# Two products of a recurrence placed beside two others, and each level's product spread over two banks

## The reference

```python
def step(s, inp):
    r_t, w_t, k_t, v_t, a_t, b_t = inp
    sa = jnp.einsum('bhvk,bhk->bhv', s, a_t)
    s = s * w_t[:, :, None, :] + sa[..., None] * b_t[:, :, None, :] + v_t[..., None] * k_t[:, :, None, :]
    y = jnp.einsum('bhvk,bhk->bhv', s, r_t) if emit else None
    return s, y
```

## Time and profile before

| | |
|---|---|
| Runs before, median (lowest to highest) | 2892.83 us (2891.24 to 2895.13), 3 runs |
| Profiled execution: its own time | 2893.22 us |
| its span, first to last instruction | 2891.4 us |
| granted TensorE clock, mean | 0.991 |
| TensorE busy | 2797.3 us, 29,030 products and as many weight loads |
| DVE, ScalarE busy | 1185.1 us, 683.0 us |

### The profile page before, as it was taken

How to read it: one execution, slowest core, us unless ns; L and a number is a source line. 1 busy time by engine, 2 the same in 40 slices (tenths; PEclk the granted TensorE clock), 3 DMA queues, 4 the chain that set the end, 5 groups by cost and what they waited for, 6 DMA issues and landing times.

```text
span 2891.4 us, 63725 instructions
## 1 busy us (share of the span) xinstructions
PE 2797.3 (97%) x29030; PEld 1683.3 (58%) x29030; DVE 1185.1 (41%) x2444; ACT 683.0 (24%) x1425; POOL 3.0 (0%) x7
## 2 busy tenths in 40 slices
PE   7999999999999999999999999989999999999997
PEld 4478777445777888864588787863333333333332
DVE  4777565445545444247786564431111011011101
ACT  2345312544322111013454126520000000000000
POOL 0000000000000000000000000000000000000000
PEclk9999999999999999999999999999999999999999
DMA  7100143212242433232000442459999999999995
GB/s 293 59 3 4 47 159 111 66 44 92 83 136 68 146 117 90 80 120 84 30 4 5 171 160 94 150 219 346 413 365 364 416 359 377 402 361 413 369 375 198
DMA packets 188787, 534.55 MB, mean 185 GB/s; under 512 B 6113, under 2 KB 80097, under 8 KB 171105
## 3 DMA queue, kind: packets, MB, share of 16 engines
q1 hardware_dynamic: 187440, 526.21, 48.6%
q0 software_dynamic: 1072, 4.19, 0.4%
HBM read 528.29 MB, written 2.10 MB: 183 GB/s over the span
## 4 chain that ended last, share of the span: by engine, by line
PE 92%; DVE 4%; ACT 1%; SPq 1%; issue 1%; DMA 1%; DVEq 0%; ACTq 0%
PE bank L572 68%; PE bank L700 12%; PE bank L1337 8%; PE bank L818 2%; PE bank L1199 1%; SPq L2990 1%; DVE WR L2456 1%; ACT ar L1627 0%; DMA rep<-in_repeated 0%; PE bank L923 0%; ACT WR L1627 0%; DVE RS L2330 0%; DVE AT L2127 0%; DVE ar L2389 0%; DVE WR L2437 0%
## 5 line engine op out<-in xcount | busy, mean ns | idle before, releaser
L572 PE MATMUL bank<-AT,WR 128*128 128x512 f32 (+1 forms) x1408 | 521.4, 521 | 5.9 <-ACT AT L1627 3.7
L1627 ACT ACTIVATE ar<-bank 128x256 f32<-128x256 f32 (+2 forms) x338 | 155.1, 463 | 1535.3 <-PE bank L572 1028.3
L572 PE MATMUL bank<-WR,ar 128*32 128x512 f32 (+1 forms) x4464 | 444.5, 555 | 1.6 <-DVE ar L2899 1.6
L572 PE MATMUL bank<-ar 128*32 128x512 f32 (+6 forms) x3990 | 429.6, 509 | 9.9 <-ACT ar L1627 5.9
L572 PEld LDWEIGHTS bank<-AT,WR 128*128 128x128 f32 x1408 | 263.0, 192 | 213.0 <-issue 196.9
L572 PEld LDWEIGHTS bank<-ar 128*32 128x32 f32 (+3 forms) x3990 | 176.1, 124 | 248.5 <-issue 237.3
L572 PEld LDWEIGHTS bank<-WR,ar 128*32 128x32 f32 x4464 | 143.7, 110 | 288.4 <-issue 285.8
L1627 ACT ACTIVATE WR<-bank 128x512 f32<-128x512 f32 (+1 forms) x224 | 122.8, 592 | 200.0 <-PE bank L572 174.7
L572 PE MATMUL bank<-AT,ar 128*32 128x512 f32 (+1 forms) x1456 | 151.5, 561 | 11.3 <-ACT AT L1627 11.3
L2909 DVE TENSOR_TENSOR YB<-YB,bank 128x512 f32<-128x512 f32 x28 | 18.0, 684 | 342.9 <-PE bank L572 342.9
L2917 DVE TENSOR_TENSOR ar<-ar,bank 128x512 f32<-128x512 f32 (+1 forms) x48 | 29.8, 621 | 286.9 <-PE bank L572 285.5
(11 more groups left out here) (368 smaller groups left out, 3287.6 us busy)
## 6 DMA issues: line engine op xcount, KB each, us to landing
WR<-in_moe_w_down SPq DMA_DIRECT2D x27, 2048.0 KB, 14.8
WR<-in_ada_w SPq DMA_DIRECT2D x20, 2048.0 KB, 8.0
ar<-in_moe_w_down SPq DMA_DIRECT2D x20, 2048.0 KB, 14.7
WR<-in_w_in SPq DMA_DIRECT2D x18, 2048.0 KB, 9.3
WR<-in_moe_w_gate SPq DMA_DIRECT2D x18, 2048.0 KB, 16.6
WR<-in_moe_w_up SPq DMA_DIRECT2D x15, 2048.0 KB, 15.9
WR<-in_moe_w_up SPq DMA_DIRECT2D x18, 1536.0 KB, 7.8
WR<-in_moe_w_gate SPq DMA_DIRECT2D x15, 1536.0 KB, 8.5
```

The lines of the kernel that those rows point to most:

```text
L572: return pe.matmul(o, lhsT, rhs, start=first, stop=last)
L1627: return act.activation(out, in_, func, **k)
```

## The change

`solve(i - 1)` is issued alternately with `level(i, 1)`, into bank 2 alone, from a third buffer `XT[2]`; the transposed values of chunk i are issued alternately with `level(i, 2)`, into bank 7. Both then use the two partition pairings that the level does not. The level's product goes to two banks, q 0 to 3 and q 4 to 7, and signals after each; `masked` is two instructions of half the width, and `inverse_doubled` waits for the first half before q = 0 and for the second before q = 4. Levels, grown and turned inverse go round over the banks 0, 1 and 6. The order within a chunk, on TensorE and on DVE, is another:

```diff
+        def level_banks(i, n):
+            return [banks[(0, 1, 6)[(5 * i + n + m) % 3]] for m in range(2)]
+        def grown_bank(i, n):
+            return banks[(0, 1, 6)[(5 * i + n + 2) % 3]]
+        def turned_bank(i, n):
+            return banks[(0, 1, 6)[(5 * i + n) % 3]]
+        solved_bank, gram_bank = banks[2], banks[7]
...
+                def value_turned(i, q, h):
+                    c = CH * (i if q < 4 else BWD[i])
+                    last = mm(pair(gram_bank, q, h), Rv[64 * h:64 * h + 64, q % 4, c:c + CH],
+                              eye[64 * h:64 * h + 64, 64 * h:64 * h + 64], True, True)
...
+                def solve(i, q, h):
+                    last = mm(pair(solved_bank, q, 1 - h), pair(XT[2], q, 1 - h), pair(G, q, 1 - h), True, True)
...
                     for q in range(8):
+                        bank = level_banks(i, n)[q // 4]
                         for h in range(2):
-                            ins = mm(pair(level_bank, q, 1 - h if n else h), pair(LTs[i % 2], q, h),
-                                     pair(X[n > 0], q, h), True, True)
-                            if (q, h) == (7, 1):
-                                ins.then_inc(S.full, 1)
+                            ins = mm(pair(bank, q, 1 - h if n else h), pair(LTs[i % 2], q, h), pair(X[n > 0], q, h), True, True)
+                        if q % 4 == 3:
+                            ins.then_inc(S.full, 1)
+                            S.done(("T1", l, i, n, q // 4))
+                        for h in range(2 if beside else 0):
+                            if beside == "solve":
+                                solve(i - 1, q, h)
+                            elif beside == "values":
+                                value_turned(i, q, h)
...
                 def inverse_doubled(i, n):
-                    pe.wait_ge(S.free, S.jobs[("T1", l, i, n)])
...
                     for q in range(8):
+                        if q % 4 == 0:
+                            pe.wait_ge(S.free, S.jobs[("T1", l, i, n, q // 4)])
...
                     if i:
                         level(i, 0)
-                        solve(i - 1)
                         inverse_doubled(i, 0)
+                        level(i, 1, "solve")
+                        inverse_doubled(i, 1)
                         y_of_chunk(i - 1, ybank)
-                        level(i, 1)
                         state(i - 1)
-                        inverse_doubled(i, 1)
-                        values_turned(i)
+                        level(i, 2, "values")
                         if i <= 4:
                             bonus(i - 1)
-                        level(i, 2)
+                        inverse_doubled(i, 2)
                         pe.wait_ge(responses_ready, seen(responses_ready))
                         against(i, 0)
-                        inverse_doubled(i, 2)
-                        against(i, 2)
                     level(i, 3, "X" if i < NCH - 1 else None)
-                    against(i, 4)
+                    against(i, 2 if i else 4)
                     inverse_doubled(i, 3)
-                    against(i, 6)
+                    against(i, 4 if i else 6)
                     level(i, 4, "LT" if i < NCH - 1 else None)
-                    if i == 0:
+                    if i:
+                        against(i, 6)
+                    else:
                         pe.wait_ge(uv_cleared, seen(uv_cleared))
                     ybank = from_state(i)
                     inverse_doubled(i, 4)
...
-                def masked(n):
-                    TT(dq(T1), step_product(banks[6]), mk(M_LEVEL + 1 + n), ALU.mult).then_inc(S.free, 1)
+                def masked(i, n):
+                    for d in range(2):
+                        bank = level_banks(i, n)[d]
+                        TT(dq(T1)[:, d], step_product(bank)[:, d],
+                           masks[:, M_LEVEL + 1 + n, d, :].unsqueeze(1).to_broadcast([128, 4, CH]), ALU.mult).then_inc(S.free, 1)
```

## The result

The changed kernel takes 2900.99 us (median of 16 runs, 2898.13 to 2904.14); the kernel before, on the same chip, 2892.85 (16 runs). The ratio is 1.0027, 95% interval [1.0020, 1.0035]: some 8 us slower, where 2882 was forecast. The profiled execution has a span of 2899.5 us against 2891.4.

The account below looks back on a forecast made before the run. TensorE's path was taken as the bound, with instruction packets a second limit (128 products each 3.5 to 4.1 us). Layer 0's -4.4 and layer 1's -6.4 us gave -10.8 from 2892.83: 2882 us, range 2870 to 2893.

Parts of the forecast that it names:

- the sum's addition for packets: Time added per chunk for TensorE's waits for instruction packets: 1.1 us without bonus work, 0.4 with, 0.3 to 0.7 elsewhere.
- The layout with its holes filled: Chunk schedule from level 0 to next level 0, before waits for packets: 20.8 us without bonus work, 22.5 with.
- both bounds: Limits on the time added for packet waits in a chunk: 0, all hidden, or a packet each 3.9 us.
- Slower: bursts: Rival: late packets stop the dense level 0 to doubling 1 chain; at 3.95 us each, +7.0 and +2.3, 2902; chance 0.08.
- part (3): Extra waits on TensorE and for the mask halves cost 0.1 to 0.2 us a chunk, at most 0.3; new banks 0.
- the first mask starts 0.70 after the level: With half-width masks, the first ends at 1.12 and doubling starts at 1.18 instead of 1.94 us after the level starts.
- The step from mask 2 to 3: Distance between the first masks of levels 2 and 3 in a chunk without bonus work, laid out as 3.1 us.
- the 4.5 named as the bound: Sign against the forecast: a step from mask 0 to mask 1 above 4.5 us would show it wrong.
- "issue" waits grow: Sign for the forecast: TensorE waits put down to issue grow from 6.3 us in two rows, still 127 to 128 products apart.
- After the recurrence everything waits for its end, so the whole difference arrives: Behind each recurrence nothing absorbs the saving, so all of the -10.8 us reaches the kernel's total time.
- Fully fed by packets: Rival: waits for packets, at 3.82 us each, replace all that was removed; 2891.5 us, no difference; chance 0.22.
- Packets cost nothing beyond today: Rival: the chunk schedule holds without additions for packet waits, 19.7 us less, 2873 us; chance 0.15.

Follow-up runs that it names:

- the swap: Changed kernel with the wait for the mask's first half written ahead of the wait for the transposed inverse's copy: 2896.96 us, ratio 1.0014.
- thin values: Changed kernel with only 2 of the 16 turned values made beside level 2 in chunks 1 to 7: 2890.41 us, ratio 0.9987.
- the fastest kernel above: Order of the kernel before, with new banks, two masks a level, turned values beside level 2 and the two waits swapped: 2888.66 us, ratio 0.9988.

## Why the prediction was wrong

**The step that failed** is the sum's addition for packets, "I add 1.1 us to a chunk without bonus, 0.4 to one with". The layout with its holes filled has 20.8 us without bonus; chunks 5 and 6 of both layers took 24.3, 23.8, 22.2 and 24.0, 23.6 in the mean. The addition had to be 2.8 us where I wrote 1.1. Of the 15.6 us by which the fourteen stretches missed (319.4 for 303.8), 11.2 stand in chunks 5 to 7. I had both bounds in hand and took, for the rate, the 3.7 us that packets had in the loose order. Dense, they come every 3.8 to 4.05 us in these chunks, and a stop of 0.8 to 1.0 us inside level 1 or doubling 2 is on the chain, as the rival "Slower: bursts" said; its 3.95 us a packet is what layer 0 shows. That rival gave 2902 for 2901, with a chance of 0.08. That its total agrees is partly luck: it put 9.3 us into the fourteen stretches, which lost 4.8. Its split is only partly right: +7.0 and +2.3 were foretold for the layers. Counted to the last doubling, which the layout includes and the stretches of the earlier trace rows do not, they are 5.6 + 1.2 = +6.8 and -0.8 + 1.2 = +0.4.

**A second step failed with it**, part (3): "The new banks are all freed by copies that the products wait for anyway: 0", and extra waits of 0.1 to 0.2 us a chunk. The kernel with the old order and one mask has the new banks, the third buffer and the waits, nothing else of the change, and is 16 us slower, over 1 us a chunk. The 2.8 us hold this miss and that of the packets together, and no run divides them: that kernel too has more stops than the kernel before (5 + 15, and 8 + 8 moved by 64, against 4 + 6). So that packets have their price is shown by the instructions added and left out; that they are all of the missing 1.7 us a chunk is not.

**What the additions hid** besides packets: (a) 0.06 us on each doubling whose mask is last, by the order of two waits; the forecast priced waits by their number (0.1 to 0.2 us a chunk) and not by which sits in front of which; shown, and worth 2 to 4 us. (b) "the first mask starts 0.70 after the level" holds for levels 0 and 2 nearly (0.93, 0.85 in the mean of layer 0), not beside gram products and behind `kept` (1.04, 1.55). The layout had the second (1.1 at level 4) but not the first. (c) The step from mask 2 to 3 was laid out with 3.1 us and took 4.55 and 4.33; with 14 of 16 values left out it is 4.08 in both layers, so some of it is packets and the rest is not separated. A small slip beside these: rates and operands, 208.81 to 212.03, are 3.22 us and not 3.15.

**Right**: the sets beside others cost no array time (PE busy 15.2 us less); 160 masks of 0.42 us; level 0 to 1 in 3.8 us, under the 4.5 named as the bound; "issue" waits grow, from 3.8 to 15.4 us in their first row, though 4.8 of these were waits for a mask, as the swap showed (10.6 left); stops 127 or 128 products apart. The distance from the last mask to doubling 4 was laid out as 3.1 us (16.6 to 19.7) and is that at the end of layer 0, 345.46 to 348.60:

```profile
347.52 1.01 PEld L829 LDWEIGHTS bank<-WR 128*64 128x64 f32 x32 [0.15 <-DVE WR L2478]
...
348.60 1.01 PEld L583 LDWEIGHTS bank<-WR 64*64 64x64 f32 x32
```

`from_state` waits for `kept(6,8)`, as foretold. In the kernel before it was 340.01 to 341.98, 2.0 us, and the products behind it ran at full clock:

```profile
341.98 1.01 PEld L572 LDWEIGHTS bank<-WR 64*64 64x64 f32 x32
...
346.13 1.15 PE L818 MATMUL bank<-WR 128*64 128x64 f32 x32 [1.16 <-ACT WR L1627]
347.21 1.13 PE L572 MATMUL bank<-AT,WR 128*128 128x512 f32 x2
```

**"After the recurrence everything waits for its end, so the whole difference arrives"** missed something. Behind layer 0 TensorE ran at a granted clock of 0.57 for a while:

```profile
349.00:353.00 4.00, 1.97 (x60) 1.70 (x58) 0.00 (x0) 2.10 (x4) 0.00 (x0) 1.00 0.00 0
353.00:357.00 4.00, 4.00 (x35) 2.62 (x36) 1.99 (x7) 0.00 (x0) 0.00 (x0) 0.57 0.29 48
```

```profile
352.93 1.74 PE L829 MATMUL bank<-WR 128*64 128x64 f32 x32 [1.33 <-ACT WR L1645]
354.60 2.08 PE L583 MATMUL bank<-AT,WR 128*128 128x512 f32 x2
```

0.6 and 0.95 us longer than the rows of before: with the 1.2 us of the later doubling that is what the stretch behind layer 0 lost. For a part of these 4 us the clock was at its lower level (1.2 GHz). The same came 6 to 8 us behind the last mask of layer 0 in five of the nine traces with the new order (the changed kernel, moved by 64, by 192, with its waits swapped, with thin values) and in three of the eleven with the old one (the kernel before moved by 128 and with the unread products, and the fastest kernel above). So it does not belong to the change alone, and that the trace of the kernel before lacks it is in part luck. Ahead of it TensorE was busy for 1.97 of 4 us, as it was in some where it did not come. Why is open.

**Fully fed by packets** (2891.5) had the mechanism and too low a price, 3.82 us. **Packets cost nothing beyond today** is refuted by the unread products. The Trainium skill, "Runtime: NRT & Kernel Launch", section "Instruction fetch mechanics", has the crossing of a block mostly hidden; the stops of 0.8 to 1.0 us each 128 products, and 13 us for 3.5 packets of added instructions, say that in a dense stretch of short products it is not.

**Sum of the 19 us** between forecast and result, in the profile: layer 0's stretch 165.3 (164.1 + 1.2) instead of 154.1, 11.2; layer 1's 156.5 instead of 149.7, 6.8; the lower clock 1.5; the rest -0.5.

**Open**: the kernel with the old order and one mask is 14 to 16 us slower than before. The wait order explains 3 to 4 of it (44 distances of 0.062 us are 2.7; the swap gave 4 in the changed kernel and was not run in this one), the placement of the kernel before perhaps 3. The rest lies in `XT[2]`, the rotating banks, the solution and the turned values now in one bank each, the added waits of level 0, doubling 0 and `from_state`, or in ScalarE, which now copies the first half of solution and values only when the second is made too; none was tried alone. The changed kernel has all of these too; what they cost in its order was not measured. The new order itself costs about 10 us: the changed kernel against the old order with two masks and the values, 1.0027 to 0.9991, though it also has `solve` beside level 1. Which of the two costs was not separated either.

## What to carry to other kernels

Where an engine runs many short instructions, count them in packets of 256 and price the dense stretch, not the mean: work that is nearly free on the array still costs its share of a packet, and in the dense stretches here leaving instructions out was worth more than hiding them. Filling holes helps only while the engine isn't the one being fed. Put the wait that ends last where it was: which of two waits stands nearest to the instruction is worth 0.06 us at each use, and a rewrite can swap them unseen. A rewrite of banks and waits that adds no work can cost more than what it makes room for (16 us here): run it alone first. Before a 0.3% difference is believed, move the whole program by a quarter packet, more than one profile each, and look at the stretch itself, since the mover costs time too.

## What the hardware showed that I had not expected

- 64 unread products' instructions a chunk, without waits and in free corners: +13 us (sure to 4) in 14 chunks, 3.7 us for each 256 instructions.
- Each of the 10 stops of the kernel before and the 22 of the changed one ends 1.2 to 1.6 us after an instruction packet has landed, and the next packet starts only 1.0 to 1.8 us later.
- The same program, its instructions moved by 64 or 128 places: the fourteen stretches take 314.6, 318.2 or 319.1 us, in one profile each.
- A wait in an instruction of its own in front of a load, instead of on the load: 0.115 us from the mask's end instead of 0.053.
- 256 waits that were long satisfied, 128 instructions at the start, bring the first product from 11.3 to 17.2 us, 384 to 24.1; 128 (64 instructions) not at all: 11.2.
- A few us at the lower clock behind layer 0's recurrence, in eight of twenty traces, of both orders.
